# Two transformer blocks on one core: three stages joined without barriers, row broadcasts from two partition groups, and VectorE's tasks in another order

## The reference

```python
# first block, twice
proj = rms_norm(x, norm1_g) @ w_in             # 3 mixers' inputs and 3 gates
x = x + (gates[0] * (y_gla @ w_br_gla) + gates[1] * (y_moba @ w_br_moba)
         + gates[2] * (y_mlstm @ w_br_mlstm)) @ w_out
x = x + square(relu(rms_norm(x, norm2_g) @ w_ff1)) @ w_ff2
# second block, layer 0 then layer 1
m = concat(conformer_conv(...), gated_deltanet(...)) @ w_out      # the mixer
x = layer_norm(ALPHA * x + m)
f = swiglu(x) if layer == 0 else sum over e of combine[e] * swiglu_e(x)   # 8 experts, top 2
x = layer_norm(ALPHA * x + f)
```

## Time and profile before

| | |
|---|---|
| times of three executions | 2663.80, 2668.48, 3192.82 us (median 2668.48) |
| profiled execution | 2669.41 us, of which 2667.6 us are its span |
| mean granted TensorE clock | 0.979 |
| PE busy | 2556.0 us (96% of the span) |
| DVE busy | 1914.3 us (72%) |
| ACT busy | 1392.4 us (52%) |
| experts (L2464), share of the chain | 30% |
| data moved | 593.19 MB, mean 222 GB/s |

### The profile page before, as it was taken

One profiled execution on the slowest core, in us unless ns is written; L12 is line 12 of the kernel. 1 busy time (PEld: TensorE's weight loads), 2 busy tenths in 40 slices (PEclk: granted clock), 3 DMA queues, 4 the chain that ended last, 5 costly groups with the idle time before them and its releaser, 6 DMA issues.

```text
span 2667.6 us, 36352 instructions
## 1 busy us (share of the span) xinstructions
PE 2556.0 (96%) x14838; PEld 2208.2 (83%) x14838; DVE 1914.3 (72%) x2215; ACT 1392.4 (52%) x1476; POOL 0.2 (0%) x4
## 2 busy tenths in 40 slices
PE   7999999899999999999999998999999999999897
PEld 7999889899898998869988867878787878788676
DVE  7765755577675545966456958888888888888787
ACT  4655444456454432224333225777777777777664
POOL 0000000000000000000000000000000000000000
PEclk9999999999999999999999998999999999999998
DMA  6334554343345544215434117999999999999796
GB/s 248 131 123 145 197 184 185 134 150 136 114 171 189 190 151 157 106 38 215 190 143 144 49 66 272 358 345 350 345 351 343 353 345 349 347 346 349 284 344 259
DMA packets 119492, 593.19 MB, mean 222 GB/s; under 512 B 17440, under 2 KB 17824, under 8 KB 77216
## 3 DMA queue, kind: packets, MB, share of 16 engines
q1 hardware_dynamic: 110096, 585.40, 59.9%
q10 hardware_dynamic: 9232, 5.47, 0.7%
HBM read 589.79 MB, written 1.05 MB: 221 GB/s over the span
## 4 chain that ended last, share of the span: by engine, by line
PE 83%; DVE 11%; ACT 3%; issue 3%; DMA 1%; DVEq 0%; POOLq 0%; ACTq 0%
PE bank L2464 30%; PE bank L576 20%; PE bank L831 12%; PE bank L1674 5%; ACT whi L650 2%; PE bank L1114 2%; PE bank L1099 2%; DVE ring_lo L807 2%; PE bank L1694 1%; PE bank L1854 1%; PE bank L2420 1%; DVE wlo L655 1%; PE bank L2483 1%; DVE big L2770 1%; PE bank L1687 1%
## 5 line engine op out<-in xcount | busy, mean ns | idle before, releaser
L655 DVE TENSOR_TENSOR wlo<-ring,whi 128x2048 fp32r<-128x2048 f32 x430 | 983.7, 2290 | 185.8 <-ACT whi L650 179.8
L650 ACT ACTIVATE whi<-ring 128x2048 fp32r<-128x2048 f32 x433 | 827.7, 1913 | 154.8 <-PE bank L2464 131.0
L2464 PE MATMUL bank<-whi,xhi 128*128 128x512 f32 x896 | 362.2, 404 | 11.0 <-DVE wlo L655 7.8
L2464 PE MATMUL bank<-whi,xlo 128*128 128x512 f32 x896 | 352.2, 393 | 0.0
L2464 PE MATMUL bank<-wlo,xhi 128*128 128x512 f32 x896 | 350.5, 391 | 0.0
L807 DVE TENSOR_TENSOR ring_lo<-ring,slot_hi 128x1024 fp32r<-128x1024 f32 x160 | 192.4, 1222 | 138.0 <-ACT slot_hi L784 130.6
L576 PE MATMUL bank<-xhi,whi 128*128 128x256 f32 x864 | 246.2, 285 | 1.9 <-DVE xlo L531 1.2
L576 PE MATMUL bank<-xlo,whi 128*128 128x256 f32 x864 | 246.1, 285 | 0.0
L576 PE MATMUL bank<-xhi,wlo 128*128 128x256 f32 x864 | 246.0, 285 | 0.0
L784 ACT ACTIVATE slot_hi<-ring 128x1024 fp32r<-128x1024 f32 x160 | 166.5, 1052 | 116.5 <-PE bank L831 81.3
L831 PE MATMUL bank<-xh,slot_hi 128*128 128x256 f32 x704 | 203.3, 289 | 3.0 <-DVE ring_lo L807 3.0
(11 more groups left out here) (500 smaller groups left out, 4645.9 us busy)
## 6 DMA issues: line engine op xcount, KB each, us to landing
ring<-in_stream SPq DMA_DIRECT2D x555, 1024.0 KB, 6.6
par<-in_par ACTq DMA_DIRECT2D x2, 2048.0 KB, 9.3
con<-in_con SPq DMA_DIRECT2D x1, 1216.0 KB, 11.3
X<-in_x SPq DMA_DIRECT2D x2, 512.0 KB, 4.2
out_y<-X SPq DMA_DIRECT2D x2, 512.0 KB, 2.6
par<-in_par ACTq DMA_DIRECT2D x2, 448.0 KB, 6.1
par<-in_par ACTq DMA_DIRECT2D x2, 157.5 KB, 2.5
con<-in_con SPq DMA_DIRECT2D x1, 64.0 KB, 4.3
```

The lines of the kernel that those rows point to most:

```text
L650: act.activation(whi[:, k % NSPLIT, :], src, ACT.Copy).then_inc(act_done, AC.step(tag + f".w{k}"))
L655: v.tensor_tensor(wlo[:, k % NSPLIT, :], src, whi[:, k % NSPLIT, :].bitcast(F32), ALU.subtract)\
L2464: mm = pe.matmul(out, left, right, start=start and i == 0, stop=stop and i == len(pairs) - 1)
```

## The change

1. `l1a` and `l1b` are `JOINED`: after them there is no barrier and the semaphores aren't cleared. Counts of `slots_used` and `slots_split` go on from one joined segment to the next (`used`, `split_by`). In place of the barrier PE waits, in `h == 0` of slot 0, for each k's `xl` by itself, and in `project(0)` of the mixer after it for each k's `xT`.
2. In a first-block layer `v_low_mixed(0)` and `(1)` come right after the sums of n = 9 and n = 10, and ACT's high halves are put in the same order.
3. In both mixers the broadcast rows are held as high and low fp32r parts in 36 partitions (`row_both`: high in 0 to 3, low in 32 to 35, zeros between), and so the selector (`sel_both`). ACT makes the high part, DVE the low part, in three places; ACT has four setup instructions more.
4. In both mixers the transposes N of half 0, A of half 0 and A of half 1 wait for `attn` instead of `kdec`; only N of half 1 waits for `kdec`.
5. In the experts the four side tasks come after the split that belongs to `up1`, and so behind `turned` and one split more.

The same diff, cut to its core (the calls that only put `used()` or `split_by()` round a count are left out):

```diff
...
 L1 = ("l1a", "l1b")
+JOINED = L1
 AHEAD = {"moe": NSPLIT - 1}
...
-            no += loops
+            no += loops if tag not in JOINED else 0
...
                 Steps.segment_now = ""
+                if tag in JOINED:
+                    return
                 if eng is not None and eng[0] != "pool":
...
                     if eng[0] == "pe" and split_from(tag):
-                        e.wait_ge(slots_used, split_from(tag))
+                        e.wait_ge(slots_used, used_ahead[tag] + split_from(tag))
                     if eng[0] == "vec" and split_from(tag) < n_slots[tag]:
-                        e.wait_ge(slots_split, n_slots[tag] - split_from(tag) - AHEAD.get(tag, 0))
+                        e.wait_ge(slots_split, split_ahead[tag] + n_slots[tag] - split_from(tag) - AHEAD.get(tag, 0))
                     e.sem_inc(arrived, 1)
...
                     pe.wait_ge(vec_done, VE.at(f"low{n}{half}"))
+                else:
+                    pe.wait_ge(vec_done, VE.at(f"next.low{n}{half}", L1[0]))
                 hi, lo_ = (y(n, half).rearrange("p (k n) -> p k n", n=UNIT) for y in (high_half, low_half))
...
                     for k in TURNED[4 * half:4 * half + 4]:
-                        if it == 0 and n == 0 and h == 0:
-                            pe.wait_ge(vec_done, VE.at(f"n1.xk{k}"))
+                        if n == 0 and h == 0:
+                            pe.wait_ge(vec_done, VE.at(f"next.xk{k}", L1[0]) if it else VE.at(f"n1.xk{k}"))
                         q = k % 4
...
                 a_slot(act, n)
-            for n in (34, 35, 36, 37, 39, 38, 40):
+            for n in (34, 35, 36, 37, 39):
                 a_high_whole(act, n)
-            for s in range(3):
-                a_high_mixed(act, s)
+            a_high_mixed(act, 0)
+            a_high_whole(act, 38)
+            a_high_mixed(act, 1)
+            a_high_whole(act, 40)
+            a_high_mixed(act, 2)
             a_high_whole(act, 41)
...
                     v_low(v, lows[n])
-            for s in range(3):
-                v_low_mixed(v, s)
+                if n in (9, 10):
+                    v_low_mixed(v, n - 9)
+            v_low_mixed(v, 2)
             v_low(v, 40)
...
                 for k in range(KD):
+                    if not last and n == 0 and h == 0:
+                        if k in (0, 1, 4, 5):
+                            pe.wait_ge(act_done, AC.at(f"next.xT{k}", L1[1]))
+                        else:
+                            pe.wait_ge(vec_done, VE.at(f"next.xT{k}", L1[1]))
                     mm = pe.matmul(PS[6 + n % 2][:, h * T:(h + 1) * T], w[:, k, h * P:(h + 1) * P], xT[:, k, :],
...
-            def broadcast(banks, row, name):
+            def broadcast(banks, j, name):
+
                 for h in range(4):
-                    mm = pe.matmul(PS[banks[h // 2]][:, (h % 2) * T:(h % 2 + 1) * T], sel[:, h, :], row,
-                                   start=True, stop=True)
+                    mm = pe.matmul(PS[banks[h // 2]][:, (h % 2) * T:(h % 2 + 1) * T], sel_both[0:36, h * P:(h + 1) * P],
+                                   row_both[0:36, j, :], start=True, stop=True)
                 mm.then_inc(pe_done, PE.step(tag + name))
...
             mm.then_inc(pe_done, PE.step(tag + "cols"))
-            broadcast((2, 3), rows[0], "bcg")
-            broadcast((0, 1), rows[1], "bcb")
+            pe.wait_ge(act_done, AC.at(tag + "sel"))
+            pe.wait_ge(vec_done, VE.at(tag + "gb.lo"))
+            broadcast((2, 3), 0, "bcg")
+            broadcast((0, 1), 1, "bcb")
             for n in range(5, 9):
...
             project(9)
-            pe.wait_ge(vec_done, VE.at(tag + "rn"))
-            broadcast((4, 5), rows[6], "bck")
-            broadcast((2, 3), rows[7], "bcq")
+            pe.wait_ge(vec_done, VE.at(tag + "kq.lo"))
+            broadcast((4, 5), 0, "bck")
+            broadcast((2, 3), 1, "bcq")
             project(10)
...
                 mm.then_inc(pe_done, PE.step(tag + f"kk{t}"))
-            broadcast((4, 5), rows[4], "bce")
+            pe.wait_ge(vec_done, VE.at(tag + "e.lo"))
+            broadcast((4, 5), 0, "bce")
             w11 = rg.take(pe).rearrange("p (k n) -> p k n", n=UNIT)
...
+            pe.wait_ge(vec_done, VE.at(tag + "attn"))
+            turn(0, 1, mNT[:, 0, :], "N")
+            turn(0, 0, mA_T[:, 0, :], "A")
+            turn(1, 3, mA_T[:, 1, :], "A")
             pe.wait_ge(vec_done, VE.at(tag + "kdec"))
-            for t in range(NT):
-                turn(t, 3 * t + 1, mNT[:, t, :], "N")
-                turn(t, 3 * t, mA_T[:, t, :], "A")
+            turn(1, 4, mNT[:, 1, :], "N")
             for t in range(NT):
...
                                ACT.Copy).then_inc(act_done, AC.step(tag + "ba" if at else None))
+            for y in (sel_both[0:36, :], row_both[0:36, :, :].rearrange("p j t -> p (j t)")):
+                act.activation(y, c("sel", 36), ACT.Copy, scale=0.0).then_inc(act_done, AC.step())
+            a_wait(act)
+            for at in (0, 32):
+                act.activation(sel_both[at:at + 4, :], c("sel", 4), ACT.Copy)\
+                   .then_inc(act_done, AC.step(tag + "sel" if at else None))
             act.wait_ge(vec_done, VE.at(tag + "pad"))
...
             def evac(n):
-                act.wait_ge(slots_used, n + 1)
+                act.wait_ge(slots_used, used(n + 1))
                 func = {"cg": ACT.Sigmoid, "z": ACT.Silu}.get(MIX_SLOTS[n][0], ACT.Copy)
...
             act.activation(rows[5][:, 0:4], rows[5][:, 0:4], ACT.Exp).then_inc(act_done, AC.step(tag + "rows"))
+            act.activation(row_both[0:4, :, :], smb[0:4, 0:2 * T].rearrange("p (j t) -> p j t", j=2), ACT.Copy)\
+               .then_inc(act_done, AC.step(tag + "gb.hi"))
             evac(3)
...
             act.activation(norms, PS[5][0:4, :], ACT.Sqrt, bias=eps_rms[0:4, 0:1]).then_inc(act_done, AC.step(tag + "l2r"))
+            act.wait_ge(vec_done, VE.at(tag + "rn"))
+            act.wait_ge(pe_done, PE.at(tag + "bcb"))
+            act.activation(row_both[0:4, :, :], norms.rearrange("p (j t) -> p j t", j=2), ACT.Copy)\
+               .then_inc(act_done, AC.step(tag + "kq.hi"))
             silu(8)
             evac(9)
+            act.wait_ge(pe_done, PE.at(tag + "bcq"))
+            act.activation(row_both[0:4, 0, :], rows[4], ACT.Copy).then_inc(act_done, AC.step(tag + "e.hi"))
             silu(9)
...
-            for t in range(NT):
-                copy(mN[:, t, :], t, 3 * t + 1, "N")
-                copy(mA[:, t, :], t, 3 * t, "A")
+            copy(mN[:, 0, :], 0, 1, "N")
+            copy(mA[:, 0, :], 0, 0, "A")
+            copy(mA[:, 1, :], 1, 3, "A")
+            copy(mN[:, 1, :], 1, 4, "N")
             for t in range(NT):
...
             v.tensor_tensor(rows[2], rows[1], rows[4], ALU.mult).then_inc(vec_done, VE.step(tag + "rows"))
+            v.wait_ge(act_done, AC.at(tag + "gb.hi"))
+            v.tensor_tensor(row_both[32:36, :, :], smb[0:4, 0:2 * T].rearrange("p (j t) -> p j t", j=2),
+                            row_both[0:4, :, :].bitcast(F32), ALU.subtract).then_inc(vec_done, VE.step(tag + "gb.lo"))
             gated(1)
...
             v.reciprocal(norms, norms).then_inc(vec_done, VE.step(tag + "rn"))
+            v.wait_ge(act_done, AC.at(tag + "kq.hi"))
+            v.tensor_tensor(row_both[32:36, :, :], norms.rearrange("p (j t) -> p j t", j=2),
+                            row_both[0:4, :, :].bitcast(F32), ALU.subtract).then_inc(vec_done, VE.step(tag + "kq.lo"))
             short_conv(8)
...
             short_conv(9)
+            v.wait_ge(act_done, AC.at(tag + "e.hi"))
+            v.tensor_tensor(row_both[32:36, 0, :], rows[4], row_both[0:4, 0, :].bitcast(F32), ALU.subtract)\
+             .then_inc(vec_done, VE.step(tag + "e.lo"))
             taps(6)
...
                  .then_inc(vec_done, VE.step())
+            VE.mark(tag + "attn")
             taps(4)
...
                 at = tag + str(p)
-                if kind == "up0" and u == 1:
+                if kind == "up1" and u == 1:
                     picks(at, p)
...
                             v.tensor_scalar(Y[:, t, :], X[:, t, :], ALPHA, None, ALU.mult).then_inc(vec_done, VE.step())
-                if kind == "up0" and u in (3, 5) and (p or rolled is not None):
+                if kind == "up1" and u in (3, 5) and (p or rolled is not None):
                     weight = wgt[:, :, p - 1] if rolled is None else wcol
                     v_scatter(v, at, u // 2 - 1, weight[:, u // 2 - 1:u // 2])
-                if kind == "up0" and u == 10 and rolled is None:
+                if kind == "up1" and u == 10 and rolled is None:
                     v_gather(v, at, (p + 1) % 2)
...
             for tag, _, loops in segs[:-1]:
+                if tag in JOINED:
+                    continue
                 for_segment(("pool", pool, None, None), tag, loops, body(tag))
...

```

42 lines of the change are left out of this document (27 added, 15 removed).

## The result

The changed kernel takes 2623.98 us (median of four executions, 2622.61 to 2624.62), the kernel before 2668.32 (median of four). The ratio is 0.9841, 95% interval 0.9824 to 0.9858. It is faster by 1.6%, clear of the spread of the runs and under the 2% named in the prediction. The forecast was 2628. One of the four executions of the kernel before took 3192.82 us; it is a slow one and stands outside the ratio. The profiled execution took 2622.61 us.

A forecast was written before the change was run, and what follows sets the result against it. TensorE's work was taken as the bound, 83% of the chain of waits. The gains 4.0 + 2.1 + 4.9 + 1.6 + 12.4 + 15.0 = 40.0 us, from 2669.4 and less 0.9, gave 2628 us, range 2613 to 2648.

The forecast's parts named there:

- the start of l1b: From l1a to l1b: PE starts on the first low part instead of waiting for POOL's clearing; 4.0 us.
- both output products: Layers 1 and 2: earlier low parts let PE start sooner; 2.1 us and, with the clock staying up, 4.9 us.
- the barrier of 1.6: From l1b to mixA: PE's 1.66 us of barrier after the transposes go; 1.6 us gained.
- the experts' term: Experts: moved side tasks no longer delay `hlo`; 1.9 us a pass in six passes, 15.0 us together.
- the mixers': Both mixers: cheaper broadcasts and earlier transposes, limited by DVE; 6.2 us each, 12.4 us together.
- the 0.85 us a pass: Experts: loss kept for what is late next, low parts and gather before the pass ends, and tasks meeting another.
- the cap's place: Mixers: DVE becomes the bound before PE's nearly 12 us come through; its waits before the transposes, 7.8 us, limit the gain.
- memory as the bound: Rival, experts: transfers set the pace, so the 15.0 us are not had; 2643 us, chance 12%.
- the dear broadcasts: Rival, mixers: matmuls with 36 rows cost as in fp32, or inline waits eat the gain; 12.4 not had, 2641, 10%.
- data waits in place of the barriers: Rival, l1b and mixA starts: the awaited steps come as late as `cleared`; 4.0 + 1.6 not had, 2634, 5%.
- The slower rival: Experts: moved tasks starve the splits, PE idles and its clock falls, 3.3 us for each of 29; 2739 us, 2%.
- The third rival: Clock stays up and DVE isn't the bound: 2627 us, or 2607 with the experts' 0.85 and PE's full mixer saving; 14%.

The follow-up runs named there:

- e2: Changed kernel with both barriers back (after l1a and after l1b) and the mixer's waits for each `xT` gone; 2628.51 us, ratio 0.9871.
- e3: Changed kernel with all low parts of the mixed sum after the last sum again, ACT's high halves in their old order; 2630.30 us, ratio 0.9875.
- e10: Changed kernel plus two unused VectorE instructions (2.4 us together) behind the split of up1 in units 7, 9 and 12 of each experts pass; 2645.68 us, ratio 0.9918.
- e11: Changed kernel with two of the four convolution taps ahead of `kdec` moved into VectorE's waits for ScalarE, in both mixers; 2623.19 us, ratio 0.9833.
- e12: e11 with the last projection's second half ahead of the wait for decayed q and the transposes of k, all taps behind `kdec`; 2615.40 us, ratio 0.9806.
- e6: Changed kernel with both mixers' broadcasts back in plain fp32 rows of four partitions, new order of the transposes kept; 2629.68 us, ratio 0.9862.
- e7: Changed kernel with the last projection's second half ahead of the transposes of k, still behind the wait for decayed q, both mixers; 2619.29 us, ratio 0.9820.

## Why the prediction was right, and where its terms were off

The forecast of 2628 lies 4 us over the measured 2624, and its mechanism held for four of the six terms to 0.2 us: the start of l1b (4.0 and 4.0), both output products (2.1 and 2.0, 4.9 and 4.8), the barrier of 1.6. e2 brings the two waits back with the sizes forecast (4.0 and 1.7), e3 layer 2's product (4.7); in layer 1, where the prediction took it from one execution that the clock stays up behind the wait, e3 loses 3.6 instead of 2.1. That the whole lies so near is in part luck: against the profile after, the experts' term is 5.8 too small and unchanged code in the first block gives 6.4 that no term has, while the mixers' is 4.6 too large. Where the terms were off:

- **Experts, 15.0 forecast, 20.8 measured.** The mis-sized term is the 0.85 us a pass kept for "what is late next": the gain is 2.8 a pass, not 1.9. In the trace of the changed kernel nothing is late next: PE is busy 124.25 of 124.30. The reason given for it was wrong though. The prediction said that a task in the new place delays only a split with a cover of 3.03; e10 gives about 1.1 at two units and at least 2.5 at a third, and it is `hlo` of the next unit that PE waits for. The tasks of 1.41 happen to stand where they leave no wait, which is why the error didn't show in the time. That is luck too: the cover was reckoned and not measured.
- **Mixers, 12.4 forecast, 7.8 measured (5.3 − 3.2 + 5.7).** That PE's saving of nearly 12 us wouldn't come through, and that DVE is the cap, held: PE now waits 3.8 us for it. The size 5.3 to 5.7 is near the 5.4 to 6.0 that stood before the transposes' part; the 0.6 for these isn't shown, and by the trace after it can't be over 0.7. What failed is the cap's place: the prediction put it in all of DVE's order up to `kdec`, and e11 shows that only the part up to the decayed q counts. It also looked for PE's new wait ahead of `bck` or `project(9)`; there PE waits 0.23, and 3.80 ahead of the transposes of k.
- **Clock.** The prediction let l1b's half clock stand and forecast none in the mixers. It is shorter after the join (1.6 us in the first slot, 1.5 in the middle of l1b), though not in e12, and it falls in mixA's states where it didn't before (−3.2). The Trainium skill, "TensorE: Matmul & The Clock Gate", section "HAM oscillation — how this bites in real kernels", has the rule by which the join would keep the clock up: PE stays warm while it is kept busy. The trace agrees in direction only; it has 0.61 over the transposes all the same, and e12's first slot takes 14.39 with the join in place.

Of the rivals, memory as the bound fell with the pass at 124.30; the dear broadcasts with 1.2 us a pair; data waits in place of the barriers with the first L852 at 505.06. The slower rival wasn't seen: e10, with nearly twice the task, lost 0.94 each on average and no clock in the pass. The third rival was right in part: l1b's clock and the experts' 0.85 a pass. Why the clock falls in mixA's states in some of these kernels and not in e6, e7 and e12 stays open. It costs 3.2 us in both profiles of the changed kernel and 1.6 in those of e2 and e10, whose mixers have the same order of work, so chance has a part in it. That it goes with what PE did just before is argued, not shown.

## What to carry to other kernels

Where an engine runs its queue in order, ask of a side task what is late next after each place in which it could stand, and measure the cover with a dummy in that very place: two runs gave 0.6 and 1.1 us at two units here, and at least 2.5 at a third. A stage in which PE and DVE take turns gives back only the saving up to the first operand that the other has to deliver; put work that needs nothing in front of that wait before shortening anything else (e12, together with `kdec` ahead of the taps). And add the clock to a wait's price: the 2.9 us wait of layer 2 cost 4.8 with the clock, and one execution of layer 1 had it without a fall.

## What the runs showed of the hardware

- The same 96 matmuls at the start of l1a took 13.80, 13.01 and 14.12 us in three executions, and at layer 1's branches the two of one and the same kernel lay 2.9 us apart. A gain of that size in one profile isn't the change's unless another profile has it.
- fp32r matmuls with 36 rows of contraction go nearly at the pace of those with 128 (0.12 each for 256 columns): 8 of them took 1.21 us at a clock of 1.00 and 4 of them 0.74, so four more cost 0.47. At a clock of 0.82 the 8 took 1.41. In plain fp32 with 4 rows the 8 took 3.71.
- Behind a wait of 3.8 or 4.7 us TensorE lost time in the matmuls as well: 4.89 instead of 3.72 us in mixA's half projection, 14.15 instead of 12.53 in l1b. Behind a wait of 2.9 us the clock fell in three of four cases (25.34, 25.23 and 24.11 us, against 22.52).
